# Six row buffers instead of seven for the first 53 gathered rows, and one weight tile kept for both chunks

## What is computed

```python
def attn_retention_mixer(xn, w_in, w_out):
    proj = xn @ w_in                      # 1024 x 3584
    ...
    return jnp.concatenate([mo, ro], axis=-1) @ w_out      # 1024 x 1024

def peer(xn, w_q, sub_keys, u, v):
    ...                                   # 8 heads, each picks 16 of 16384 experts for a token
    hid = gelu(einsum('td,thkd->thk', tc, u[ec]))
    return einsum('thk,thkd->td', gc * hid, v[ec])
```

## Time and profile before

| what | us |
|---|---|
| median of 3 runs | 2176.43 (2174.74 to 2179.7) |
| the profiled execution, its own time | 2174.65 |
| its span in the trace | 2172.8 |
| busy: TensorE / VectorE / ScalarE / GpSimd | 1852.1 / 1305.9 / 493.4 / 687.8 |

### The profile page before, as it was taken

How to read it: one execution, slowest core, us unless ns; L and a number is a source line. 1 busy time by engine, 2 the same in 40 slices (tenths; PEclk the granted TensorE clock), 3 DMA queues, 4 the chain that set the end, 5 groups by cost and what they waited for, 6 DMA issues and landing times.

```text
span 2172.8 us, 19255 instructions
## 1 busy us (share of the span) xinstructions
PE 1852.1 (85%) x5978; PEld 888.7 (41%) x5978; DVE 1305.9 (60%) x3327; ACT 493.4 (23%) x1232; POOL 687.8 (32%) x593
## 2 busy tenths in 40 slices
PE   9999998997899998989877887777978767888875
PEld 4445554333245445445433333333433433334322
DVE  1343433221022767677587797987777898777764
ACT  1232221111111224222222222212112222222221
POOL 2110001110000334444344344554334445444442
PEclk9999999999999999999988998889999988999999
DMA  7432229999786999999999999999999999999996
GB/s 262 155 121 96 112 101 377 415 418 419 319 355 236 374 400 374 418 420 421 421 421 421 421 418 398 422 408 421 421 421 413 398 418 418 422 420 422 418 415 255
DMA packets 115081, 781.44 MB, mean 360 GB/s; under 512 B 16080, under 2 KB 17792, under 8 KB 21664
## 3 DMA queue, kind: packets, MB, share of 16 engines
q0 software_dynamic: 78928, 542.37, 60.7%
q1 hardware_dynamic: 32544, 227.75, 26.0%
q10 hardware_dynamic: 3504, 10.04, 1.2%
HBM read 782.20 MB, written 10.49 MB: 365 GB/s over the span
## 4 chain that ended last, share of the span: by engine, by line
DMA 32%; DVE 15%; issue 14%; POOL 6%; PE 5%; ACT 0%; POOLq 0%; DVEq 0%; ACTq 0%
DMA arena<-in_c_rows_dram,arena 32%; DVE arena L2707 6%; POOL arena L2809 6%; PE banks L1815 2%; DVE x L2717 2%; PE banks L2693 1%; DVE arena L2601 1%; DVE arena L2604 1%; DVE arena L2610 1%; PE banks L1906 1%; DVE arena L2639 1%; PE banks L2325 1%; DVE arena L2643 0%; DVE arena L2607 0%; DVE arena L2646 0%
## 5 line engine op out<-in xcount | busy, mean ns | idle before, releaser
L2693 PE MATMUL banks<-arena 128*128 128x512 f32 x1784 | 884.0, 641 | 238.5 <-ACT arena L2774 238.1
L2809 POOL DMA_INDIRECT arena<-in_c_rows_dram,arena x512 | 610.0, 1191 | 819.0 <-PE banks L2693 579.0
L2707 DVE CUSTOM_DVE_ANT_0 arena<-arena,xn 128x1024 f32<-128x1024 f32 x512 | 625.7, 1223 | 297.4 <-DMA arena<-in_c_rows_dram,arena 292.0
L2693 PEld LDWEIGHTS banks<-arena 128*128 128x128 f32 x1784 | 345.6, 203 | 712.8 <-issue 356.1
L2774 ACT ACTIVATE arena<-ident,small 128x128 f32<-128x128 f32 x446 | 158.2, 395 | 548.2 <-DVE small L2714 534.7
L313 PE MATMUL banks<-ring,hT 128*128 128x512 f32 (+1 forms) x480 | 200.4, 573 | 0.0
L375 ACT COPY arena<-banks 128x512 f32<-128x512 f32 (+4 forms) x218 | 101.2, 493 | 292.5 <-PE banks L359 113.2
L2765 ACT ACTIVATE small<-small 128x2 f32<-128x2 f32 x256 | 52.1, 204 | 495.1 <-DVE small L2707 495.0
L313 PEld LDWEIGHTS banks<-ring,hT 128*128 128x128 f32 x480 | 87.3, 190 | 99.0 <-issue 97.3
L401 POOL TENSOR_TENSOR small<-small 128x1 f32<-128x1 f32 (+4 forms) x24 | 33.5, 1397 | 297.4 <-DVE small L397 271.5
L2398 PE MATMUL banks<-ring,hT 128*128 128x512 f32 x176 | 86.5, 595 | 0.0
(11 more groups left out here) (313 smaller groups left out, 1779.5 us busy)
## 6 DMA issues: line engine op xcount, KB each, us to landing
arena<-in_c_experts_dram SPq DMA_DIRECT2D x53, 1024.0 KB, 25.5
ring<-in_c_experts_dram SPq DMA_DIRECT2D x33, 1024.0 KB, 22.9
ring<-in_c_w_in_dram SPq DMA_DIRECT2D x30, 1024.0 KB, 4.8
ring<-in_c_odd_w_in_dram SPq DMA_DIRECT2D x19, 1024.0 KB, 11.3
ring<-in_c_w_q_dram SPq DMA_DIRECT2D x18, 1024.0 KB, 11.8
ring<-in_c_even_w_in_dram SPq DMA_DIRECT2D x12, 1024.0 KB, 18.3
arena<-in_c_even_w_in_dram SPq DMA_DIRECT2D x10, 1024.0 KB, 10.7
arena<-in_c_rows_dram,arena POOLq DMA_INDIRECT x512
```

The costliest lines, as they stand in the source:

```text
L2693: r = e.matmul(banks[:, bank_of[("acc", L, c, hf)], :], diag[:, diag_of[m], :], rows[:, row_of[m], D + hf * 512:D + (hf + 1) * 512], start ...
L2707: e.tensor_tensor_reduce(u, u, xn[:, c, :], 1.0, 0.0, ALU.mult, ALU.add, hid3[:, c, h, k:k + 1]).then_inc(ve.sem, ve.up(("u", p)))
L2809: e.indirect_dma_start(rows[:, b, :], None, table_uv, bass.IndirectOffsetOnAxis(ap=eix[:, c, 16 * h + k:16 * h + k + 1], axis=0)).then_inc ...
```

## The change

Six row buffers (0 to 5) go round for the first 53 rows. Place `NSLOT + 6`, the seventh's, gets the output weight tile (0, 0) at the start of the mixer and keeps it until chunk 1 has used it at position 49; from row 53 on it is a row buffer too, so there are nine as before. The load of that tile for chunk 1 is gone. The other tiles have other places, and so are issued after other products.

```diff
         def join_tile(c, c0, k):
-            return ("join again", c0, k) if c else ("join", c0, k)
+            return ("join again", c0, k) if c and (c0, k) != (0, 0) else ("join", c0, k)
...
             bring(0, 2048, 0, NSLOT + 5)
-            bring(0, 2048, 4, NSLOT + 6)
-            bring_join(0, 0, 0, NSLOT + 3)
+            bring(0, 2048, 4, NSLOT + 3)
+            bring_join(0, 0, 0, NSLOT + 6)
...
             bring(1, 0, 0, NSLOT + 5)
-            bring(1, 0, 4, NSLOT + 6)
-            load(e, ("wq", 0, 0), a["c_w_q"][0, 0], NSLOT + 3)
-            load(e, ("wq", 0, 1), a["c_w_q"][0, 1], NSLOT + 4)
-            bring(1, 512, 0, NSLOT + 1)
-            bring(1, 512, 4, NSLOT + 2)
-            bring(1, 1536, 0, NSLOT + 5)
-            bring(1, 1536, 4, NSLOT + 6)
+            bring(1, 0, 4, NSLOT + 3)
+            load(e, ("wq", 0, 0), a["c_w_q"][0, 0], NSLOT + 4)
+            load(e, ("wq", 0, 1), a["c_w_q"][0, 1], NSLOT + 1)
+            bring(1, 512, 0, NSLOT + 2)
+            bring(1, 512, 4, NSLOT + 5)
+            bring(1, 1536, 0, NSLOT + 4)
+            bring(1, 1536, 4, NSLOT + 1)
             bring(1, 2048, 0, NSLOT + 3)
-            bring(1, 2048, 4, NSLOT + 4)
+            bring(1, 2048, 4, NSLOT + 2)
...
             load(e, ("wq", 0, 4), w_q[0, 4], 2)
-            load(e, join_tile(1, 0, 0), w_e_out[0], 3)
+            load(e, join_tile(1, 0, 4), w_e_out[1], 3)
             load(e, ("wq", 0, 5), w_q[0, 5], 4)
-            load(e, join_tile(1, 0, 4), w_e_out[1], 5)
-            load(e, join_tile(1, 512, 0), w_e_out[2], 3)
-            load(e, join_tile(1, 512, 4), w_e_out[3], 5)
+            load(e, join_tile(1, 512, 0), w_e_out[2], 5)
+            load(e, join_tile(1, 512, 4), w_e_out[3], 3)
...
-        free, last_in, row_of, row_before = [0, 1, 2, 5, 6, 3, 4], {}, [], []
+        free, last_in, row_of, row_before = [0, 5, 4, 1, 3, 2], {}, [], []
         for m in range(LAST):
             if m == MORE:
-                free[:0] = [7, 8]
+                free[:0] = [7, 8, 6]
...
-        first_tile = {1: ("again", 512, 0), 2: ("again", 512, 4), 3: ("again", 2048, 0), 4: ("again", 2048, 4),
-                      5: ("again", 1536, 0), 6: ("again", 1536, 4)}
+        first_tile = {1: ("again", 1536, 4), 2: ("again", 2048, 4), 3: ("again", 2048, 0), 4: ("again", 1536, 0),
+                      5: ("again", 512, 4), 6: ("join", 0, 0)}
```

## The result

In the first comparison the changed kernel took 2193.55 us (5 runs, 2189.63 to 2198.02) against 2177.65 us: ratio 1.0073, 95% interval 1.0057 to 1.0089, +15.9 us. Forecast was +5.45. The profiled execution took 2195.08 us, its span is 2193.3 us; that of the kernel before, 2174.65 us, was 3.0 us faster than the median of its five runs. So the two traces lie 20.4 us apart, further than the medians do, and sizes read from them alone are too large.

The account below looks back on a forecast made before the run. The prediction took the DMA engines as the bound, full from 870 us. Late rows 7.95, missing load -2.50 and tile places 0 gave +5.45 us on the median 2176.43, so 2181.9 us; own range 2178.5 to 2186, wider range 2174.5 to 2190.5.

Parts of the forecast that it names:

- What bounds the kernel: From 870 to 1300 us all DMA engines are full at 420 GB/s, so DMA time lost earlier never comes back.
- The sign that was named: From 735 to 870 us: DMA share falls by 0.04 to 0.06, VectorE's row waits grow from 36.4 to over 42 us.
- The bare time of a row: A row finding the DMA queue empty takes 6.06 us from request to use, read from row 39.
- The skill's estimate of 4.4 us: Rule of about 2 us fixed plus bytes at 436 GB/s per row; by it the sum would be about 0.
- the last three groups: Late rows around 30, 38 and 52, with nothing to fill the DMA gaps, add up to 7.45 us lost.
- How late requests become: With six buffers row m waits for value product m - 6; late rows before 879 us lose 7.95 us of DMA time.
- Rival 3: All five groups of late rows count whole and late rows delay later requests: 14.15 - 2.50 = +11.7 us, 2188.1; chance 0.12.
- the five groups: Late rows around 14, 24, 30, 38 and 52, at 4.01, 2.69, 1.85, 3.19 and 2.41 us; whole, 14.15 us.
- One load less: The output tile not loaded falls in 872.83 to 888.3 us, in the full DMA stretch: -2.50 us, ends -2.5 and nothing.
- Other places of tiles: One more tile in the empty 700 to 709 us against rows 1 to 5 asked for later: 0, ends -2.50 and +2.3.
- 2: Faster: TensorE bounds 735 to 870 us, late rows never make it wait, two tiles won: -5.0 us, 2171.4; chance 0.10.
- 1: Shortage partly absorbed: the last late rows leave some 2.5 us, which the missing load pays; 2176.4, the same; chance 0.22.

Follow-up runs that it names:

- six_only: Kernel before with six row buffers instead of seven until row 53, tiles' old places and all loads kept; 1.0053 of the kernel before, +11.5 us.
- after_again: The changed kernel itself, unaltered, measured a second time against the kernel before; ratio 1.0051 (1.0039 to 1.0064), +11.1 us.
- new_places_seven: Changed kernel with output tile (0, 0) loaded again and seven row buffers from the start; 0.9987 of the kernel before, -2.8 us.
- after_split: Changed kernel with score products of heads 2 to 5 moved behind their position's value products; 1.0033 of the kernel before, +7.2 us.
- after_warm_all: Changed kernel with extra 128x128 products before score products of heads 2 to 5 and value pairs of rows 2 to 53; 1.0076 of the kernel before.

## Why the prediction was right in its direction and wrong in its size

The sum 7.95 - 2.50 + 0 had two terms that failed: the time that six buffers lose before row 53 was put at 7.95 us and measured 11.5, and the tile that isn't loaded was credited with 2.50 us that don't show in the changed kernel.

1. **What bounds the kernel, right.** DMA time lost before row 53 never came back: 19.0 us at row 53, 20.4 at the last row, and the same in 17 of 18 traces (table in the section on the parts of the change). The sign that was named held in kind and not in size: the DMA share from 735 to 870 us fell from 0.98 to 0.89, by 0.09 instead of 0.04 to 0.06, and VectorE's waits grew to 54.4 us.
2. **The bare time of a row, nearly right.** 6.06 us forecast; rows 24, 38 and 52 took 6.00, 6.49 and 5.73, rows 22 and 23 5.56 and 5.57, so 6.06 was up to 0.5 us too long. The skill's estimate of 4.4 us (Trainium skill, "SBUF — State Buffer", "The DMA setup-cost knee") isn't seen in any of them, and the loss that it would have explained away is there. (By that estimate the last three groups would have left 2.47 us, not 2.54; the sum stays near 0.) Rows 14 and 30, at 8.9 and 8.6, were outside the 5.5 to 6.6 that I gave.
3. **How late requests become: the direction right, the term mis-sized.** This is the step that failed: "How late VectorE gets the row = shift of the request + 6.06 - ...", where I took the shifts from the old trace, as if TensorE made its value products at the old times. The late row makes its own value product late and that the request six rows on; where a score product stands ahead of the values, a later row does it as well. Row 22 shows it: 7.3 us of shift by the old trace, 16.5 in the new one, behind value product 16, which waited with the score product for row 19. The groups were also chosen by the old trace: at rows 12 and 22, set aside as smaller, the new one has its longest waits for a row, 4.77 and 5.56 us. 7.95 us forecast for it, 11.5 (8.3 to 14.6) measured by `six_only`. By rows: 0.5 forecast up to row 20 and 1.7 (-0.2 to +3.7) measured, 7.45 behind and 8.5 (5.7 to 11.3) measured. So neither part is far off alone, and 7.95 lies just outside the interval of the whole; `six_only` puts the term at about 1.4 times what I took. Rival 3 had said that a late row delays its own value product and so closes the circle; its mechanism is the one that the rows show. Its 14.15 us for the five groups are within the interval of `six_only`, and its sum of +11.7 is what `after_again` measured, but with a credit for the tile that isn't seen, and the first groups, which it counts whole at 6.7 us, cost 1.7: the agreement is in part luck.
4. **One load less: near with seven buffers, not seen with six.** -2.50 forecast; -2.0 by itself, none to be seen in the changed kernel. The full stretch begins 30 us later there, so the tile falls out of a stretch with some room; that this took the whole credit is not shown. I took 870 us over from the old trace as the start of the full stretch, though my own first term moved it.
5. **Other places of tiles, right.** 0 forecast with ends -2.5 and +2.3; nothing to be seen with six buffers, and -2.8 with seven, just beyond the end. The empty 9 us took two tiles, where I had one: 233 GB/s from 700 to 709 us in the changed kernel, 2.1 MB.

```profile
700.00:709.00 9.00, 8.23 (x49) 6.19 (x50) 7.01 (x31) 1.19 (x4) 0.00 (x0) 1.00 0.64 233
```

6. **The sum.** 11.5 with no credit for the load is what `after_again` measures (+11.1). The first comparison has some 4 us more. The two intervals overlap (from 1.0057 there, up to 1.0064 here), no run explains the difference, and it stays open.
7. **Rivals.** 2 is refuted: TensorE wasn't the bound, late rows made it wait (24.8 us for 11.7). 1 is refuted by size. Not foreseen at all: the drops of TensorE's clock, for which the runs show no cost clear of the noise.

What stays open: how the value products' lateness goes round, by parts. The runs speak against the clock and the score product as what six buffers add; that it is the waits for the rows themselves is what is left, not what a run isolates.

## What to carry to other kernels

When a buffer is taken from a ring whose request waits for the use of an earlier item, its price goes round: take the old trace for the first late item only, since every time behind it moves with it; here the whole came out at 1.4 times what the old trace gave. Look for the place where a saved transfer falls out once more after the losses are costed: that it counts only where the DMA engines are still full is argued here, not shown. Compare several traces before a size is read from one: here `new_places_seven`, 2.8 us faster than the kernel before by its ratio, was profiled 4.0 us behind it at row 53. In an in-order engine, whatever waits for a later item should stand behind the work that frees the buffers of earlier ones; here that alone gave 4 us of 2178, in both kernels.

## What the runs showed of the hardware

TensorE's granted clock fell to 0.5, the 1.2 GHz level, for 6.8 us in all in the profiled stretch of the kernel before and 23.9 in the changed one. Each of the seven falls in these two came at or next to the end of a wait of 2.06 us or more (3.00 us, then value products of 6.06 us instead of 3.60). Not every such wait brought one: in `after_split` the clock stayed at full after 2.34 us, and the value products took 3.70:

```profile
772.51 3.70 PE L2700 MATMUL banks<-arena 128*128 128x512 f32 x8 [2.34 <-ACT arena L2781]
```

The changed kernel had 23.9 us at the lower level in one execution and 17.1 in another (`after_again`). Removing nearly all of it with extra products (3.4 us left in `after_warm_all`) made nothing faster.

A gathered row of 1.05 MB that found the queue empty took 5.56 to 6.49 us from its request on GpSimd to its use on VectorE (rows 22, 23, 24, 38 and 52 of the changed kernel).
